# The last block's first two products on un-normalised x, in banks of their own, and squares added on VectorE

## What is computed

```python
for i in range(2):
    x = x + mixer_i(rmsnorm(x, norm_mix[i]))
    x = x + conv_ffn(rmsnorm(x, norm_ffn[i]), ...)

mod = silu(c) @ ada_w + ada_b                    # shift, scale, gate: one vector each
h = rmsnorm(x, norm_g) * (1 + scale) + shift
p = h @ w_in                                     # all input columns, in blocks of 256
c_val, c_gate, c_og, ts, r_og, g_conv, g_rwkv = split(p)
# ts = r, k, v (1024 each) and two 64-wide low-rank parts; each is shifted by a token:
z + mu * (prev - z)                              # prev of token 0 is 0
# decay and a come from tanh(w_low) @ w2 and a_low @ a2; then an RWKV-7 scan,
# a 31-tap convolution branch, two output products, w_out, x + gate * out, a last rmsnorm
```

## Time and profile before

| | us |
|---|---|
| median of 3 runs | 1065.82 (1065.8 to 1066.68) |
| the profiled execution | 1065.15 |
| its span, first to last instruction | 1063.4 |
| PE busy | 1034.2 (97%) |
| DVE busy | 841.8 (79%) |
| ACT busy | 614.8 (58%) |

### The profile page before, as it was taken

One profiled execution on the slowest core, in us unless ns is written; L12 is line 12 of the kernel. 1 busy time (PEld: TensorE's weight loads), 2 busy tenths in 40 slices (PEclk: granted clock), 3 DMA queues, 4 the chain that ended last, 5 costly groups with the idle time before them and its releaser, 6 DMA issues. The chain is left out here.

```text
span 1063.4 us, 25136 instructions
## 1 busy us (share of the span) xinstructions
PE 1034.2 (97%) x10788; PEld 987.6 (93%) x10788; DVE 841.8 (79%) x1388; ACT 614.8 (58%) x879; POOL 18.4 (2%) x38
## 2 busy tenths in 40 slices
PE   7999999999999999999999988999999999999997
PEld 6999999999999989999999978889999988889997
DVE  7965689887879886988888757889899899965473
ACT  7744664444446666544444567556568566686443
POOL 2000000000000000000000000000000000000000
PEclk9999999999999999999999999999999999999999
DMA  9652266766564515585765636234233332234531
GB/s 285 209 186 82 78 220 218 237 228 233 201 199 151 174 41 179 166 276 197 250 222 173 202 114 192 88 120 120 89 113 121 95 107 81 82 119 150 170 120 41
DMA packets 135928, 168.21 MB, mean 158 GB/s; under 512 B 3200, under 2 KB 125056, under 8 KB 135584
## 3 DMA queue, kind: packets, MB, share of 16 engines
q1 hardware_dynamic: 131936, 153.44, 44.7%
q0 software_dynamic: 3904, 13.50, 3.4%
HBM read 164.83 MB, written 2.10 MB: 157 GB/s over the span
## 5 line engine op out<-in xcount | busy, mean ns | idle before, releaser
L308 PE MATMUL bank<-xh,wh 128*128 128x256 f32 x1360 | 397.4, 292 | 0.6 <-DVE wl L270 0.6
L309 PE MATMUL bank<-xl,wh 128*128 128x256 f32 x1392 | 393.5, 283 | 0.0
L310 PE MATMUL bank<-xh,wl 128*128 128x256 f32 x1360 | 384.4, 283 | 0.0
L308 PEld LDWEIGHTS bank<-xh,wh 128*128 128x128 f32 x1360 | 260.0, 191 | 10.7 <-issue 3.6
L309 PEld LDWEIGHTS bank<-xl,wh 128*128 128x128 f32 x1392 | 266.6, 192 | 0.6 <-issue 0.5
L310 PEld LDWEIGHTS bank<-xh,wl 128*128 128x128 f32 x1360 | 260.2, 191 | 0.0
L270 DVE TENSOR_TENSOR wl<-raw,wh 128x2048 fp32r<-128x2048 f32 x95 | 216.8, 2286 | 45.3 <-ACT wh L265 45.2
L265 ACT ACTIVATE wh<-raw 128x2048 fp32r<-128x2048 f32 x95 | 181.0, 1907 | 38.9 <-PE bank L633 35.5
L294 DVE TENSOR_TENSOR wl<-raw,wh 128x1024 fp32r<-128x1024 f32 x86 | 103.6, 1217 | 19.1 <-ACT wh L286 19.0
L2451 DVE SCALAR_TENSOR_TENSOR hf<-big,vecs,hf 128x256 f32<-128x256 f32 x240 | 101.3, 477 | 0.0
L286 ACT ACTIVATE wh<-raw 128x1024 fp32r<-128x1024 f32 x86 | 87.6, 1057 | 11.2 <-PE bank L310 5.5
(11 more groups left out here) (405 smaller groups left out, 2195.9 us busy)
## 6 DMA issues: line engine op xcount, KB each, us to landing
raw<-in_ffn_w_up SPq DMA_DIRECT2D x44, 1024.0 KB, 5.1
raw<-in_w_in SPq DMA_DIRECT2D x36, 1024.0 KB, 5.5
raw<-in_ffn_w_down SPq DMA_DIRECT2D x22, 1024.0 KB, 5.0
big<-in_ada_w_t POOLq DMA_DIRECT2D x24, 512.0 KB, 5.1
raw<-in_gla_w_in SPq DMA_DIRECT2D x11, 1024.0 KB, 5.5
raw<-in_attn_w_qkv SPq DMA_DIRECT2D x6, 1024.0 KB, 4.9
raw<-in_gla_w_out SPq DMA_DIRECT2D x4, 1024.0 KB, 5.4
raw<-in_attn_w_out SPq DMA_DIRECT2D x4, 1024.0 KB, 5.3
```

Source lines behind the costliest of these rows:

```text
L308: nc.tensor.matmul(ps, wh, xh, start=start, stop=False)
L309: nc.tensor.matmul(ps, wh, xl, start=False, stop=False)
L310: return nc.tensor.matmul(ps, wl, xh, start=False, stop=stop)
```

## The change

- **Last block's opening.** Blocks `N_L3` and `N_L3 + 1` are multiplied with `EARLY[4]`, the split of x times (1 + scale) times norm weight, which gets two more columns that hold the shift: 258 columns per matmul instead of 256, each half block in a PSUM bank of its own (banks 2 and 1, 4 and 5). The squares are summed within the first of them. DVE multiplies the result by `RS` (`scaled`), keeps the shift's product as a bias, and ACT finishes (`take_shifted`). Block `N_L3 + 2` uses the normalised, shifted `XH`, `XL` as before; `lora()` moves into its middle and uses three fp32r matmuls per tile with split weights (`WLH` on ACT, `WLL` on DVE). The pass of line 1360 goes.
- **Order behind it.** ACT loads the Sigmoid table right after `RS`; the table load of `keys_scaled(0)` goes. ACT does the first pair's sigmoids and `keys_scaled(0)` before it takes v0. On DVE `front(0, 3)` and the use of v0 stand ahead of the remainder in slot 3 of step -2.
- **First mixer.** For heads 0 to 2 DVE adds the two tiles of squares (`squares_added`), and `gla_sums` is one matmul instead of two.

The core of the diff:

```diff
@@ PE, first mixer
-                for v in range(2):
+                if h < GH_ - 1:
+                    pe.wait_ge(sem("gla_squares_added"), h + 1)
+                for v in range(1 if h < GH_ - 1 else 2):
@@ DVE, first mixer
+            def squares_added(h):
+                dve.wait_ge(sem("gla_squares"), h + 1)
+                v.tensor_tensor(GSQ[h][:, 0, :], GSQ[h][:, 0, :], GSQ[h][:, 1, :], ALU.add)\
+                    .then_inc(sem("gla_squares_added"), 1)
@@ PE, last block
+            def early_last(j, banks, summed):
+                n, (eh, el) = N_L3 + j, EARLY[4]
+                pe.wait_ge(w_lo_ready, n + 1)
+                for m in range(2):
+                    ms = slice(m * P, (m + 1) * P)
+                    for k in range(KT):
+                        if summed and m == 0 and k % 2 == 0:
+                            pe.wait_ge(sem("early_split"), 16 + k // 2 + 1)
+                        last = three(PS[banks[m]][:, 0:T + 2], WH[:, n % RING, k, ms], WL[:, n % RING, k, ms],
+                                     eh[:, k, :], el[:, k, :], k == 0, k == KT - 1)
...
             def lora():
-                pe.wait_ge(sem("shift_added"), 1)
+                pe.wait_ge(sem("lora_steps"), 1)
                 for k in range(KT):
-                    last = nc.tensor.matmul(PS[3][:, 0:T], w_lora[:, k, :], HF[:, k, :], start=k == 0, stop=k == KT - 1)
+                    last = three(PS[3][:, 0:T], WLH[:, k, :], WLL[:, k, :], XH[:, k, :], XL[:, k, :], k == 0, k == KT - 1)
...
+            early_last(0, (2, 1), True)
+            early_last(1, (4, 5), False)
+            for u in range(8):
+                if u < 4:
+                    pe.wait_ge(sem("rms_split"), 16 + u + 1)
+                if u == 4:
+                    lora()
+                unit(N_L3 + 2, u)
@@ ACT
-            squares(4)
+            early(4, lambda k: mod[:, 24 + k:25 + k])
+            split_hi(act, N_L3 + 2)
             norm_split(4, modulate=True)
+            act.wait_ge(sem("lora_landed"), 48)
+            nc.scalar.activation(WLH, w_lora, ACT.Copy).then_inc(sem("lora_hi"), 1)
+            take_shifted(0)
+            split_hi(act, N_L3 + 3)
+            take_shifted(1)
             act.wait_ge(sem("lora_rows"), 1)
+            nc.scalar.activation(Z, PS[3][:, 0:T], ACT.Copy).then_inc(sem("lora_taken"), 1)
+            split_hi(act, N_L3 + 4)
+            act.wait_ge(sem("lora_steps"), 2)
             nc.scalar.activation(LORA[0:64, :], LORA[0:64, :], ACT.Tanh).then_inc(sem("lora_ready"), 1)
...
-            for n in range(N_L3, N_L3 + 3):
-                split_hi(act, n + 2)
-                take_block(n)
+            loaded[0] = "sigmoid"
+            front(0, 0)
             keys_scaled(0)
+            take_block(N_L3 + 2)
@@ DVE
+            lo(N_L3 + 2)
...
+            norm(4, last_mix, modulate=True)
+            scaled(0)
+            dve.wait_ge(sem("lora_hi"), 1)
+            v.tensor_tensor(WLL, w_lora, WLH.bitcast(F32), ALU.subtract).then_inc(sem("lora_steps"), 1)
+            scaled(1)
...
+            use_shifted(0)
+            lo(N_L3 + 3)
+            dve.wait_ge(sem("lora_taken"), 1)
+            v.tensor_tensor(LORA[:, 1:T], Z[:, 0:T - 1], Z[:, 1:T], ALU.subtract)
+            ch.step(v.tensor_scalar(LORA[:, 0:1], Z[:, 0:1], -1.0, None, ALU.mult))
+            v.scalar_tensor_tensor(LORA, LORA, vec("rwkv_mu_2", 24), Z, ALU.mult, ALU.add)\
+                .then_inc(sem("lora_steps"), 1)
+            use_shifted(1)
...
+            lo(N_L3 + 4)
...
+                    if (s, r) == (-2, 3):
+                        front(0, 3)
+                        use_block(N_L3 + 2)
                     slot(s, r)
-                    if s + 2 < 8:
+                    if s + 2 < 8 and (s, r) != (-2, 3):
                         front(s + 2, r)
```

More of the change, by code:

```diff
@@ L981, in _ @@
             mlp(1, N_F1, E_F1)
-            sums(4)
+            def early_last(j, banks, summed):
[8 more added lines that the diff above has]
+                                     eh[:, k, :], el[:, k, :], k == 0, k == KT - 1)
+                        if summed and m == 0 and k % 2:
+                            pe.wait_ge(sem("squares_ready"), 16 + k // 2 + 1)
+                            for kk in (k - 1, k):
+                                sums_done = nc.tensor.matmul(PS[3][:, 0:T], ones, HF[:, kk, :], start=kk == 0,
+                                                             stop=kk == KT - 1)
+                            if k == KT - 1:
+                                sums_done.then_inc(sem("square_sums"), 1)
+                last.then_inc(block_done, 1)
             def lora():
                 pe.wait_ge(sem("lora_landed"), 48)
-                pe.wait_ge(sem("shift_added"), 1)
+                pe.wait_ge(sem("lora_steps"), 1)
                 for k in range(KT):
-                    last = nc.tensor.matmul(PS[3][:, 0:T], w_lora[:, k, :], HF[:, k, :], start=k == 0, stop=k == KT - 1)
+                    last = three(PS[3][:, 0:T], WLH[:, k, :], WLL[:, k, :], XH[:, k, :], XL[:, k, :], k == 0, k == KT - 1)
                 last.then_inc(sem("lora_rows"), 1)
             def bank_freed(n):
-                if n < N_L3 + 2:
+                if n < N_L3 + 3:
                     return
@@ L1345, in norm_split @@
                     return
+                if modulate:
+                    nc.scalar.preload_act_table(ACT.Sigmoid)
                 if then is not None:
@@ L2283, in _ @@
             lo(N_QKV + 2)
-            norm(2, lambda k: vec(*second_mix(k)), between=first_keys)
+            norm(2, second_mix, between=first_keys)
             def qk_norm(e):
@@ L2388, in _ @@
[L2388 to L2394, removed]
+            norm(3, second_ffn, between=lambda: first_val(N_F1))
+            last_mix = lambda k: mod[:, 24 + k:25 + k]
@@ new lines, in _, with use_shifted @@
+            norm(4, last_mix, modulate=True)
[3 more added lines that the diff above has]
+            scaled(1)
+            def use_shifted(j):
+                dve.wait_ge(evacuated, taken(N_L3 + j))
+                for m in range(2):
+                    ins = v.scalar_tensor_tensor(RKV[:, 8 * j + m, :], U[:, j, m, 0:T], vec("rwkv_mu_2", 8 * j + m),
+                                                 RKV[:, 8 * j + m, :], ALU.mult, ALU.add)
+                ins.then_inc(sem("shifted"), 1)
```

96 lines of the change are left out of this document (56 added, 40 removed).

## The result

| | before | after |
|---|---|---|
| median | 1065.81 us (1065.71 to 1066.68, 4 runs) | 1056.32 us (1056.08 to 1057.35, 4 runs) |
| the profiled execution | 1065.15 | 1056.08 |
| its span | 1063.4 | 1054.3 |
| PE busy | 1034.2 (97%) | 1030.4 (98%) |

The ratio is 0.991, with an interval of 0.9898 to 0.9922: 9.5 us faster by the medians, 9.1 by the two profiled executions. The forecast was 1057.7 with a range of 1055.5 to 1061.5, so it held, 1.4 us on the cautious side.

A forecast was written before the change was run, and what follows sets the result against it. TensorE, busy 97%, bounds the kernel, so idle time and removed matmuls count. 1.3 (mixer) + 6.8 (last block, to `kr_ready`) = 8.1 off 1065.15 gives 1057.0 profiled; the median, 0.67 above, 1057.7; range 1055.5 to 1061.5 us.

The forecast's parts named there:

- First mixer: Three matmuls, six records of 0.216 us, leave TensorE: 1.3 us gained; the additions on VectorE cost 0.
- TensorE's own work at the seam: Last block's opening: r0 and k0 end at T+15.0, v0 at T+23.7; the 258 columns add 0.1 us in all.
- T: The moment TensorE is done with the second network and takes up the last block, 612.87 us before the change.
- rival of a second pass: Last block's opening: 258 columns double the 0.12 us matmul step, making it slower, 1068.0 us; chance 0.04.
- The norm and the low-rank product: Last block: norm from T+8.4, hidden under TensorE's work; low-rank weights split at T+17.6, 0.3 us before they are wanted.
- Pre-activations: Last block: gate0's load takes 8.6 us, landing T+22.5; its split delays Tanh, so they start T+24.8 against T+30.5 before.
- Three transfers share: Rival at the last block's loads: r1's load delays gate0's by 3.1 us, giving 1060.8 us; chance 0.12.
- Tables: Last block: early Sigmoid load costs nothing; rival: Tanh and Sigmoid each load one, 1.28 us before Tanh, 1059.0 us, chance 0.12.
- Step -2: Last block: two TensorE waits go, but VectorE's chain to `kr_ready` grows from 8.6 to 10.55 us, ending at T+39.8.
- the given-back wait: TensorE reaches step -1 at T+38.2 but `kr_ready` comes at T+39.8: about 1.6 us of the gain lost.
- the 1.70: TensorE's 1.70 us wait at step -2's key sums goes: sigmoids and scaled keys done near T+27.2, wanted at T+28.5.
- The 0.96: TensorE's 0.96 us wait at its next sum in step -2 goes, with 2.2 us of units as cover.

The follow-up runs named there:

- the doubled store: The changed kernel with x stored a second time, to a spare tensor, between the first store and gate0's load: 1060.93 us.
- the gap filled: The kernel before with nine more plain f32 matmuls, results unused, in TensorE's 3.88 us gap behind the last block's sums: 1065.23 us.
- `kr_ready` first: The changed kernel with the product that gives kr_ready put ahead of slot 9's half remainder in step -2 on VectorE: 1055.24 us.
- three parts undone: The changed kernel with the mixer's sums, VectorE's order in slot 3 of step -2 and v0's place on ScalarE as before: 1057.62 us.
- gate0's load first: The changed kernel with gate0's load issued ahead of the wait for the norm and the store of x: 1055.98 us.

## Why the prediction was right, point by point

- **First mixer: 1.3 forecast, 1.29 measured** (M), and 1.32 and 1.26 with the part alone removed or added. The covers on VectorE held.
- **TensorE's own work at the seam.** r0 and k0 were to end at T+15.0 and end at T+14.99. The step of the 258-column matmuls is 0.12: r0 and k0 with the sums take 0.05 more than 9.18 of the earlier trace rows and 48 steps of 0.12; by columns it was to be 0.1. The rival of a second pass is out.
- **The norm and the low-rank product.** The norm was put at T+8.4 and starts at T+8.24; TensorE waits for none of its parts, nor for `lora()`'s weights.
- **Pre-activations: T+24.8 forecast, T+23.95 measured.** Here is the mis-sized term. Gate0's load was to land at T+22.5. ScalarE's split of it starts at 633.39, T+21.68: the load was issued at 625.48, T+13.77 for the T+13.9 assumed, and took 7.9 us, not the 8.6 of the earlier trace rows. The row was of one transfer, and I took it without a range. TensorE's wait there is 0.17, not 1.1, and the load issued ahead of the store (it lands in 5.7 us, long before it is needed) gains 0.2, not 1.0. That the load stands on the path was right, as the doubled store shows.
- **Three transfers share: rejected.** Gate0's load landed in 7.9 us with r1's right behind it; r1's took the delay itself (11.2 us from issue to landing).
- **Tables: right.** No load ahead of Tanh; without the early one P grows by 1.43, where 1.3 was forecast.
- **Step -2: the sum right, the reasons partly wrong.** The chain on VectorE was forecast at 10.55 us from the key sums to `kr_ready` and measures 10.49, the given-back wait at 1.6 and measures 1.63. The sigmoids and scaled keys are done at T+26.33 (T+27.2 forecast), 1.2 us before TensorE wants them, so the 1.70 is gone as forecast. The reasons are where it is weak. The place of v0 on ScalarE has no part in it. The early table load, the sigmoids ahead of the half split, and an opening that leaves ScalarE early are left, and no run separates them. The 0.96 goes by VectorE's order (2.13 and 1.23 without it), but that wait was harmless to begin with: it lies beside VectorE's chain, which is what step -1 waits for, and moving the remainder behind the chain's start puts it inside the chain. The prediction did price that; it did not say that the two moves, v0's and VectorE's, bring nothing together.
- **The idle clock.** The prediction named the 1.2 GHz level behind the gap and counted it implicitly, in the whole stretch from T to T+30.5. By itself it was worth 0.5 us on the path in one execution and 1.4 in another (P of 30.01 with the gap filled, against 30.49 and 31.42), and 1.2 by the medians. So the gain depends on which execution of before it is counted from; the changed kernel has no such gap.
- **Sum.** 8.1 forecast, 9.1 measured between the profiled executions: 1.29 in M and 7.94 in S and E, less 0.13 by which the changed execution was later at M's start. `kr_ready` comes at T+38.67 and not at T+39.8. Of these 1.1 us, 0.85 were there at the pre-activations, 0.17 came from there to the chain's start (4.23 for the 4.4 assumed) and 0.06 in the chain.

## What to carry to other kernels

Where one seam of a kernel already has the form that the change gives to another, its rows price the new one to a few tenths. In a stretch where two engines run level, don't count a removed wait until you have followed the other engine's chain to the point where they meet: of the two waits that went in step -2, neither needed v0 taken late, and one was moved to step -1, as the piece of weight work that was put "behind" the chain's start was inside it. To gain there, work that nobody needs yet has to go behind the chain's *end*, as the kernels from `kr_ready` first onward do. And when a part is taken back to see what it was worth, look whether all of it is back: the kernel with three parts undone still had most of ScalarE's new order.

## What the runs showed of the hardware

- The price of one and the same idle gap of 3.9 us before a dense stretch varied between executions: the granted clock stood at the 1.2 GHz level for 3.4 us in one and for 6.8 in another. Waits of 1.6 to 2.1 us left it at the 2.4 GHz level in every profiled execution, one of 3.34 us did not and cost 1.5 us more. Unprofiled executions of the kernels with waits of 1.6 and 2.13 us had mean granted clocks of 0.997 against 0.999 and were about 1 us slower, so the shorter waits may not be free each time.
- A 1 MB load issued 0.4 us behind a 1 MB store took 7.7 to 8.6 us to land (7.7 for r1's in the kernel with gate0's load first), where the median is 5.5. One issued right behind both, r1's in the changed kernel, took 11.2, and one behind two stores took 10.6.
- Matmuls of 258 columns kept a step of 0.120 us (48 of them from 620.92 to 626.70 in the changed kernel), as those of 256 behind them (24 from 626.70 to 629.57).
